# Head distances from two fp32r products with dA split in a high and a low part, in a two-layer hybrid decoder trunk

## The chip, the cores and the metric

One core of a Trainium2 chip. The metric is the device time of one execution in microseconds. The kernel before ran in 1644.17 us (median of 3 runs, 1643.96 to 1645.16).

## The reference

A decoder trunk of two layers on 256 tokens with 1024 features, all in float32. A layer is a half-step SwiGLU FFN, a mixer (an mLSTM branch with 4 heads beside a Mamba-2 SSD branch with 32 heads in 4 groups), a second FFN, and a gated per-layer embedding. The part that the change touches is the decay between positions in the SSD branch, in chunks of 128 tokens:

```python
acs = jnp.cumsum((dt * a_neg).reshape(bsz, nc, L, ng, ne), axis=2)
ah = jnp.transpose(acs, (0, 1, 3, 4, 2))
causal = jnp.tril(jnp.ones((L, L), dtype=bool))
decay = jnp.exp(jnp.where(causal, ah[..., :, None] - ah[..., None, :], -jnp.inf))
cb = jnp.einsum('bctgn,bcsgn->bcgts', cc, bc)
y_intra = jnp.einsum('bcgts,bcgets,bcsgep->bctgep', cb, decay.astype(x.dtype), xw)
...
y_inter = (jnp.einsum('bctgn,bcgepn->bctgep', cc, s_start.astype(x.dtype))
           * jnp.exp(acs)[..., None].astype(x.dtype))
```

## The kernel before

The five engines have one instruction list each, written out by hand, and meet at semaphores; there is no planner. SyncE loads weights. TensorE (PE) does the products, ScalarE (ACT) and VectorE (DVE) convert and evacuate, GpSimd (POOL) does a few masks and products.

**Units.** All weights come in units of 1 MB in a ring of three. For each unit ACT makes the rounded high part w_hi (L499, fp32r) and DVE the rest w_lo (L787); PE then computes three fp32r products for each block, hi by hi, hi by lo and lo by hi (`feat` L1316, `tok` L1328 to L1330 with 256 columns; `wide` and `tall` through L1342 to L1344 with 512). A unit of 48 instructions in the mixer is `feat` or `tok`.

**A layer's mixer** has 4 groups, `body(g, first)`, the first of which is written out and the others run in a loop. A group is 9 units: BC, QK, X01, X23, V, Z0, Z1, O, GA. Between them PE does the small work of the group. G counts the groups over both layers. Units 2 ahead are converted by `step(p)` on ACT and DVE.

**Distances.** dA = -softplus(dt) * exp(a_log) stands for all tokens and heads in one tile (DVE L931, once a layer, in `softplus_gates`). For chunk c and half (four heads of the group's eight) POOL builds R = tri_le * dA, 128 by 512 float32 (`distances_of` L402 to L406; the instruction is L404). PE multiplies it by the strict triangle (`segments` L1479, the product is L1482) and gets the sums of dA between two positions in bank 4 + 2c + half; ACT's exp (`decay` L599, L602) turns them into seg. For chunk 1 PE also multiplies by ones (`from_start` L1485, product L1488), which gives the sums from the chunk's start; ACT's exp (L610) makes cs. All these products have float32 operands. The two tiles R lie in the memory of xwe and of zth.

**Order around it in a steady group** (the second to fourth of a layer). On POOL: the tiles of chunk 0 were built at the end of the group before, after `yi_done` and `zth_ready` (L451 to L455); those of chunk 1 follow when `seg_done` says that PE has read chunk 0 (L431 to L433). Then the masks pm (L438), seg (L444) and cs (L448), the ysum addition (L458) after `ysq_ready`, and small copies for the next group (L413 to L419). On PE (L1583 to L1608): `segments(0,0)` in the middle of the second half of QK, `segments(0,1)` behind QK, `segments(1,0)` within X01, `segments(1,1)` behind it, the scores, X23, the first half of V, `from_start`, the rest of V, and so on; `outputs(1)` behind O signals `y_done`. On DVE: w_lo of X01 and X23, evacuation of BC, its convolution (L994 and L997: eight instructions on SBUF tiles), q and k (L1053, L1055), w_lo of V, the score distances pm (L1024, after PE's scores), w_lo of Z0, evacuation and convolution of X01, and so on; V's evacuation is L1067; at the end L1148 and L1153 make y. On ACT: tanh of the first convolution (L597), w_hi of V, exp of chunk 0, w_hi of Z0, tanh, exp of chunk 1.

**In the first group** of a layer the list is another: `small` and `small_back` bring the gate inputs, DVE's `softplus_gates` makes dA, PE waits for it in `gates` (L1453, L1454), then DVE does w_lo of V, `gate_rows` (L935 to L963: copies, scans and small steps on 4 partitions), w_lo of Z0, X01. POOL builds chunk 0 right after `dA_ready`. ACT copies cst (L667), which PE's `memory_read` (L1527) takes.

Merging after the groups (L1639 to L1651) runs `feat` on ha_hi, ha_lo and on yb_hi, yb_lo, which lie at `base` in the memory that the group's tiles had.

Of the kernel before, what the change touches and what calls it, by code (L numbers as in the profile page):

```python
# [5 lines left out]
F32 = mybir.dt.float32  # L6
F32R = mybir.dt.float32r
BF16 = mybir.dt.bfloat16
ALU = mybir.AluOpType
# [3 lines left out]
P = 128  # L13
# [10 lines left out]
def trunk(nc, T, out):  # L24
    DEPTH, D, FF = T["w1_ffn1"].shape
    S = T["x"].shape[1]
    CH = 128
    NC = S // CH
# [45 lines left out]
    with ctx:  # L74
# [4 lines left out]
        def at(name, shape, dt, off):  # L79
            n = 1  # L80
            for d in shape[1:]:
                n *= d
            n *= 2 if dt == BF16 else 4
            return nc.alloc_sbuf_tensor_at(name, shape, dt, offset=off), off + (n + 31) // 32 * 32

        def sb(name, shape, dt=F32):
            t, top[0] = at(name, shape, dt, top[0])
            return t

        raw = [sb(f"w_raw{i}", [P, KD, NP]) for i in range(RING)]  # L90
        whi = [sb(f"w_hi{i}", [P, KD, NP], F32R) for i in range(RING)]
# [14 lines left out]


        ident = sb("ident", [P, P])
        tri_le = sb("tri_le", [P, P])
# [9 lines left out]
        spx = sb("spx", [P, NC, 36])  # L119
        dA = sb("dA", [P, NC, SH])  # L120
        e_a = sb("e_a", [P, SH])
        dcol = sb("dcol", [P, SI // P])
# [26 lines left out]
        a = base  # L149
        seg, a = at("seg", [P, NC, EH, P], F32, a)  # L150
        xcv, a = at("xcv", [P, 4, S], F32, a)
        bcv, a = at("bcv", [P, 2, S], F32, a)
# [5 lines left out]
        cth, a = at("cth", [P, 2, S], F32, a)  # L158

        late = a  # L160
        xw, a = at("xw", [P, NC, EH * HP], F32, a)
        xwe, a = at("xwe", [P, EH * HP], F32, a)
# [5 lines left out]
        st, a = at("st", [P, EH * HP], F32, a)  # L168
        xin, a = at("xin", [P, 2, 2, S + 3], F32, a)
        zth, a = at("zth", [P, 2, S], F32, a)  # L170
        R = (xwe[:, :].rearrange("p (e t) -> p e t", e=4),
             zth[:, :, :].rearrange("p a b -> p (a b)").rearrange("p (e t) -> p e t", e=4))
        vtok, a = at("vtok", [P, NC, 258], F32, a)
# [25 lines left out]

        a5 = late  # L200
        r_i, a5 = at("r_i", [MH, S], F32, a5)
        r_f, a5 = at("r_f", [MH, S], F32, a5)
        r_b, a5 = at("r_b", [MH, S], F32, a5)
        r_w, a5 = at("r_w", [MH, S], F32, a5)
        pre_row, a5 = at("pre_row", [40, S], F32, a5)
        sp_a, a5 = at("sp_a", [P, NC, 36], F32, a5)
# [26 lines left out]
        def rows(x):  # L233
# [7 lines left out]
             u_hi_ready u_lo_ready silu_done prod_done h1_hi_ready h1_ready small_done x_abs sp_exp  # L241
            dA_ready ea_ready cum_done cum_exp row_tr row_ready row_back tok_ready r_built seg_done exp_done
            conv_done tanh_done cv_ready scores_done d_ready p_exp pm_ready sct_ready cb_done cbm_done
# [131 lines left out]
        def _(pool):  # L375
# [23 lines left out]
            def row_norm(n):  # L399
                power(n + 1, "var_ready", var[:, :], "rms_ready", rms[:, :])  # L400

            def distances_of(g, c, half):  # L402

                g_.tensor_tensor(R[half][:, :, :], tri_le[:, :].unsqueeze(1).broadcast_to([P, 4, P]),  # L404
                                 dA[:, c, bass.ds(g * EH + 4 * half, 4)].unsqueeze(2).broadcast_to([P, 4, P]),
                                 ALU.mult).then_inc(sem["r_built"], 1)  # L406

            def group(lay, g, first, last):
# [16 lines left out]
                if first:  # L425
                    pool.wait_ge(sem["dA_ready"], lay + 1)
                    for half in range(2):
                        distances_of(g, 0, half)
                else:
                    token_columns()  # L430
# [20 lines left out]
                if not last:  # L451
                    pool.wait_ge(sem["yi_done"], G + 1)
                    pool.wait_ge(sem["zth_ready"], G * 2 + 2)
                    for half in range(2):
                        distances_of(g + 1, 0, half)  # L455

# [317 lines left out]
        def _(dve):  # L774
# [120 lines left out]
            def softplus_gates(lay):  # L895
# [23 lines left out]
                for n in (15, 13, 11, 9, 7, 5, 3):  # L919
# [12 lines left out]
                                        in1=e_a[:, :].unsqueeze(1).broadcast_to([P, NC, SH]),  # L932
                                        op0=ALU.mult, op1=ALU.mult).then_inc(sem["dA_ready"], 1)

            def gate_rows(lay):  # L935
# [240 lines left out]

            dve.wait_ge(sem["const_ready"], 2)
            for c in range(NC):
                dve.wait_ge(sem["in_loaded"], 16 * NC)
                dve.sem_inc(sem["h_ready"], 2)  # L1180
# [113 lines left out]
        def _(pe):  # L1294
# [172 lines left out]
            def groups(lay):  # L1467
                def body(g, first):
# [10 lines left out]
                    def segments(c, half):  # L1479

                        pe.wait_ge(sem["r_built"], G * 4 + (2 * c + half + 1))
                        mm(bank[4 + 2 * c + half][:, :], tri_gt[:, :], R[half][:, :, :], start=True, stop=True)\  # L1482
                            .then_inc(sem["seg_done"], 1)

                    def from_start():  # L1485
                        for half in range(2):
                            pe.wait_ge(sem["exp_done"], G * 4 + (3 + half))
                            mm(bank[6 + half][:, :], ones[:, :], R[half][:, :, :], start=True, stop=True)\  # L1488
                                .then_inc(sem["seg_done"], 1)
# [259 lines left out]
```

## Time and profile before

| | |
|---|---|
| median of 3 runs | 1644.17 us (1643.96 to 1645.16) |
| time of the profiled execution | 1645.88 us |
| its span, first to last instruction | 1644.1 us |
| busy: PE, DVE, ACT, POOL | 1601.2, 1047.4, 730.1, 205.4 us |
| mean granted TensorE clock | 0.994 |

Busy time is the time in which an engine has an instruction running. Matmuls overlap, so for PE the distance from one start to the next tells what an instruction costs, not its own duration.

### The profile page before, as it was taken

What the parts mean: (1) busy time and instruction counts of PE and PEld (TensorE: products, weight loads), DVE (VectorE), ACT (ScalarE), POOL (GpSimd) and SP (SyncE); (2) the same over time, 40 slices, a digit from 0 to 9 for tenths busy, and PEclk for the clock granted to TensorE, in tenths of its full rate; (3) what the DMA queues carried; (4) which work ended last, traced back from release to release, by engine and by line L of the source; (5) the groups of instructions that cost most, each with busy time, mean ns of one, the idle gap of its engine ahead of it and who ended that gap; (6) DMA issues with size and microseconds to landing.
All of it is one profiled execution on the core that took longest, in us unless ns stands there. A gap on an engine that the chain in (4) does not pass through costs nothing.

```text
span 1644.1 us, 24426 instructions
## 1 busy us (share of the span) xinstructions
PE 1601.2 (97%) x9792; PEld 1399.9 (85%) x9792; DVE 1047.4 (64%) x1282; ACT 730.1 (44%) x880; POOL 205.4 (12%) x178
## 2 busy tenths in 40 slices
PE   7999989999999999999999999999999999999997
PEld 5888878999999978888778887899999999788885
DVE  5445488878777645454665545888787765554545
ACT  5444444444345345443554345344444543544444
POOL 1000013353330000000000000243343200000000
PEclk9999999999999999999999999999999999999999
DMA  7565634454545556555455654345453465466551
GB/s 238 182 201 179 171 111 129 129 165 126 170 128 180 180 166 198 194 184 184 157 186 184 193 179 142 115 129 153 156 152 117 140 204 193 149 203 197 184 180 64
DMA packets 245237, 270.85 MB, mean 165 GB/s; under 512 B 12504, under 2 KB 226360, under 8 KB 245176
## 3 DMA queue, kind: packets, MB, share of 16 engines
q1 hardware_dynamic: 239472, 266.90, 52.0%
q10 hardware_dynamic: 5704, 3.13, 0.7%
q8 instruction: 40, 0.66, 0.2%
q14 instruction: 21, 0.17, 0.0%
HBM read 268.94 MB, written 1.05 MB: 164 GB/s over the span
## 4 chain that ended last, share of the span: by engine, by line
PE 90%; DVE 5%; ACT 2%; issue 2%; DMA 0%; POOL 0%; SPq 0%; POOLq 0%; DVEq 0%; ACTq 0%
PE bank L1316 31%; PE bank L1342 16%; PE bank L1343 16%; PE bank L1344 16%; PE bank L1482 1%; DVE w_lo L787 1%; PE bank L1384 1%; PE bank L1330 1%; PE bank L1329 1%; PE bank L1328 1%; PE bank L1686 1%; ACT w_hi L499 1%; DVE xcv L997 1%; PE bank L1544 1%; PE bank L1488 1%
## 5 line engine op out<-in xcount | busy, mean ns | idle before, releaser
L787 DVE TENSOR_TENSOR w_lo<-w_raw,w_hi 128x2048 fp32r<-128x2048 f32 x252 | 586.8, 2330 | 292.4 <-ACT w_hi L499 292.4
L499 ACT ACTIVATE w_hi<-w_raw 128x2048 fp32r<-128x2048 f32 x252 | 481.3, 1913 | 228.8 <-PE bank L1344 116.2
L1316 PE MATMUL bank<-u_hi,w_hi 128*128 128x256 f32 x1152 | 341.7, 297 | 2.5 <-DVE u_lo L822 2.5
L1316 PE MATMUL bank<-u_lo,w_hi 128*128 128x256 f32 x1152 | 328.1, 285 | 0.0
L1316 PE MATMUL bank<-u_hi,w_lo 128*128 128x256 f32 x1152 | 328.1, 285 | 0.0
L1316 PEld LDWEIGHTS bank<-u_hi,w_hi 128*128 128x128 f32 x1152 | 223.1, 194 | 9.3 <-issue 7.8
L1316 PEld LDWEIGHTS bank<-u_lo,w_hi 128*128 128x128 f32 x1152 | 223.3, 194 | 5.1 <-issue 4.8
L1316 PEld LDWEIGHTS bank<-u_hi,w_lo 128*128 128x128 f32 x1152 | 223.0, 194 | 0.0
L1342 PE MATMUL bank<-w_hi,u_hi 128*128 128x512 f32 x416 | 166.8, 401 | 5.5 <-DVE u_lo L822 4.1
L1342 PE MATMUL bank<-w_hi,ha_hi 128*128 128x512 f32 x416 | 165.1, 397 | 3.5 <-DVE w_lo L787 3.4
L1344 PE MATMUL bank<-w_hi,u_lo 128*128 128x512 f32 x416 | 163.4, 393 | 0.0
L1343 PE MATMUL bank<-w_lo,u_hi 128*128 128x512 f32 x416 | 163.0, 392 | 0.0
L1344 PE MATMUL bank<-w_hi,ha_lo 128*128 128x512 f32 x416 | 162.5, 391 | 0.0
L1343 PE MATMUL bank<-w_lo,ha_hi 128*128 128x512 f32 x416 | 162.0, 390 | 0.0
L397 POOL TENSOR_TENSOR rms<-var,m_half 128x2 f32<-128x2 f32 x11 | 7.7, 696 | 1074.5 <-DVE var L815 1061.3
L1342 PE MATMUL bank<-w_hi,h_hi 128*128 128x512 f32 x352 | 139.1, 395 | 0.4
L1343 PE MATMUL bank<-w_lo,h_hi 128*128 128x512 f32 x352 | 138.5, 393 | 0.0
L1344 PE MATMUL bank<-w_hi,h_lo 128*128 128x512 f32 x352 | 136.9, 389 | 0.0
L553 ACT ACTIVATE h_hi<-bank 128x512 fp32r<-128x512 f32 x44 | 26.3, 598 | 165.4 <-PE bank L1384 165.4
L1342 PEld LDWEIGHTS bank<-w_hi,u_hi 128*128 128x128 f32 x416 | 78.7, 189 | 22.1 <-DVE w_lo L787 5.9
L1342 PEld LDWEIGHTS bank<-w_hi,ha_hi 128*128 128x128 f32 x416 | 78.1, 188 | 21.0 <-DVE w_lo L787 5.3
L1344 PEld LDWEIGHTS bank<-w_hi,u_lo 128*128 128x128 f32 x416 | 78.7, 189 | 17.0
(260 smaller groups left out, 2496.5 us busy)
## 6 DMA issues: line engine op xcount, KB each, us to landing
w_raw<-in_w_ffn_dram SPq DMA_DIRECT2D x264, 512.0 KB, 4.4
w_raw<-in_w_in_dram SPq DMA_DIRECT2D x160, 512.0 KB, 4.8
w_raw<-in_w_branch_b_dram SPq DMA_DIRECT2D x32, 512.0 KB, 4.1
w_raw<-in_w_branch_a_dram SPq DMA_DIRECT2D x16, 512.0 KB, 4.4
w_raw<-in_w_out_dram SPq DMA_DIRECT2D x16, 512.0 KB, 4.0
w_raw<-in_w_ple_gate_dram SPq DMA_DIRECT2D x16, 512.0 KB, 4.3
y_feat<-in_w_ple_dram ACTq DMA_DIRECT2D x2, 1024.0 KB, 5.1
h<-in_x_dram SPq DMA_DIRECT2D x2, 512.0 KB, 4.8
```

The source lines that it names most:

```text
L499: a_.activation(whi[slot][:, :, :], raw[slot][:, :, :], ACT.Copy).then_inc(sem["w_hi"], 1)
L553: a_.activation(h1_hi[b][:, :, :], two(6 - 2 * b), ACT.Copy).then_inc(sem["h1_hi_ready"], 1)
L787: v_.tensor_tensor(wlo[slot][:, :, :], raw[slot][:, :, :], whi[slot][:, :, :].bitcast(F32), ALU.subtract).then_inc(sem["w_lo"], 1)
L997: ins = v_.scalar_tensor_tensor(out=dst[:, q, :], in0=src, scalar=gcw[:, j, t:t + 1], in1=dst[:, q, :], op0=ALU.mult, op1=ALU.add)
L1316: i = mm(o, w[slot][:, k, cs], x[:, k, :], start=(k + q == 0 and not seeded), stop=(k == KD - 1 and q == 2 and not seeded), skip_group_che ...
L1328: mm(o, xh[:, k, cs], whi[slot][:, k, :], start=(k == 0), stop=False)
L1329: mm(o, xh[:, k, cs], wlo[slot][:, k, :], start=False, stop=False)
L1330: i = mm(o, xl[:, k, cs], whi[slot][:, k, :], start=False, stop=(k == KD - 1))
L1342: mm(o, xh, wh, start=start, stop=False, skip_group_check=True)
L1343: mm(o, xh, wl, start=False, stop=False, skip_group_check=True)
L1344: return mm(o, xl, wh, start=False, stop=stop, skip_group_check=True)
L1384: i = nc.tensor.transpose(bank[6 - 2 * b][:, k * S + c * P:k * S + (c + 1) * P], h1f[:, c, k * P:(k + 1) * P], ident[:, :])
```

## The change

dA is split, once a layer, in dA_hi, rounded to fp32r, and dA_lo, the rest rounded. The strict triangle and ones get fp32r copies. POOL builds R_hi and R_lo in place of R, and PE makes two fp32r products for each float32 one. R_hi lies where R lay (xwe and zth), R_lo in xw's memory. xw is read by `outputs`, so for the next group's chunk 0 POOL builds R_lo only after `y_done`. The gate rows that lay in xw's memory go to xcv's. The new operands of PE are placed at 64 modulo 256 bytes, and all that lies behind them moves.

```diff
+        def place(off, n):
+            return off + (n - off) % 256
...
+        top[0] = place(top[0], 64)
+        tri_gt_r = sb("tri_gt_r", [P, P], F32R)
+        ones_r = sb("ones_r", [P, P], F32R)
         ident = sb("ident", [P, P])
...
         dA = sb("dA", [P, NC, SH])
+        dA_hi = sb("dA_hi", [P, NC, SH], F32R)
+        dA_lo = sb("dA_lo", [P, NC, SH], F32R)
...
+        a = place(a, 64)
         late = a
+        xwe_at = late + NC * EH * HP * 4
...
+        a = place(a, 64)
+        zth_at = a
         zth, a = at("zth", [P, 2, S], F32, a)
-        R = (xwe[:, :].rearrange("p (e t) -> p e t", e=4),
-             zth[:, :, :].rearrange("p a b -> p (a b)").rearrange("p (e t) -> p e t", e=4))
+        R_hi = [at(f"R_hi{b}", [P, 4, P], F32R, off)[0] for b, off in enumerate((xwe_at, zth_at))]
+        R_lo = [at(f"R_lo{b}", [P, 4, P], F32R, late + b * 4 * P * 4)[0] for b in range(2)]
...
-        a5 = late
+        a5 = xcv_at
         r_i, a5 = at("r_i", [MH, S], F32, a5)
...
+            def part_of(dst, part, g, c, half):
+
+                return g_.tensor_tensor(
+                    dst[half][:, :, :], tri_le[:, :].unsqueeze(1).broadcast_to([P, 4, P]),
+                    part[:, c, bass.ds(g * EH + 4 * half, 4)].bitcast(F32).unsqueeze(2).broadcast_to([P, 4, P]), ALU.mult)
+
             def distances_of(g, c, half):
-                g_.tensor_tensor(R[half][:, :, :], tri_le[:, :].unsqueeze(1).broadcast_to([P, 4, P]),
-                                 dA[:, c, bass.ds(g * EH + 4 * half, 4)].unsqueeze(2).broadcast_to([P, 4, P]),
-                                 ALU.mult).then_inc(sem["r_built"], 1)
+                part_of(R_hi, dA_hi, g, c, half)
+                part_of(R_lo, dA_lo, g, c, half).then_inc(sem["r_built"], 1)
...
-                    pool.wait_ge(sem["dA_ready"], lay + 1)
+                    pool.wait_ge(sem["dA_split"], lay + 1)
...
                     for half in range(2):
-                        distances_of(g + 1, 0, half)
+                        part_of(R_hi, dA_hi, g + 1, 0, half)
+                    pool.wait_ge(sem["y_done"], G + 1)
+                    for half in range(2):
+                        part_of(R_lo, dA_lo, g + 1, 0, half).then_inc(sem["r_built"], 1)
...
+                dve.wait_ge(sem["dA_ready"], lay + 1)
+                ch.add(v_.tensor_copy(dA_hi[:, :, :], dA[:, :, :]))
+                ch.wait()
+                v_.tensor_tensor(dA_lo[:, :, :], dA[:, :, :], dA_hi[:, :, :].bitcast(F32), ALU.subtract)\
+                    .then_inc(sem["dA_split"], 1)
...
+            ch.add(v_.tensor_copy(tri_gt_r[:, :], tri_gt[:, :]))
+            ch.add(v_.tensor_copy(ones_r[:, :], ones[:, :]))
...
-                        mm(bank[4 + 2 * c + half][:, :], tri_gt[:, :], R[half][:, :, :], start=True, stop=True)\
+                        mm(bank[4 + 2 * c + half][:, :], tri_gt_r[:, :], R_hi[half][:, :, :], start=True, stop=False)
+                        mm(bank[4 + 2 * c + half][:, :], tri_gt_r[:, :], R_lo[half][:, :, :], start=False, stop=True)\
                             .then_inc(sem["seg_done"], 1)
...
-                            mm(bank[6 + half][:, :], ones[:, :], R[half][:, :, :], start=True, stop=True)\
+                            mm(bank[6 + half][:, :], ones_r[:, :], R_hi[half][:, :, :], start=True, stop=False)
+                            mm(bank[6 + half][:, :], ones_r[:, :], R_lo[half][:, :, :], start=False, stop=True)\
                                 .then_inc(sem["seg_done"], 1)
```

By the sizes of the tiles, `base` lies at 128 modulo 256 bytes before and at 0 after; the weights' ring, u_hi, u_lo, ha_hi and ha_lo stay at 192.

## Rows read from the trace of the kernel before

**Rows 1.** The page's chain that ended last, share of the span by engine.
```profile
PE 90%; DVE 5%; ACT 2%; issue 2%; DMA 0%; POOL 0%; SPq 0%; POOLq 0%; DVEq 0%; ACTq 0%
```

**Rows 2.** PE's groups by line (busy us, mean ns); then its timeline (start, length).
```profile
L1482 PE MATMUL bank<-xwe,tri_gt 128*128 128x512 f32 x32 | 16.4, 592 | 0.0
L1488 PE MATMUL bank<-xwe,ones 128*128 128x512 f32 x16 | 8.8, 631 | 0.0
...
254.98 1.02 PE L1482 MATMUL bank<-xwe,tri_gt 128*128 128x512 f32 x2
...
256.70 0.50 PE L1496 MATMUL bank<-bcv 128*128 128x128 f32 x3
```

**Rows 3.** PE's waits: for whom, us in total, times, longest.
```profile
PE bank L1454 <- DVE dA L931: 7.6, 2, 3.8
PE bank L1337 <- DVEq L1180: 6.9, 1, 6.9
```

**Rows 4.** PE's timeline in an FFN, the first and the 35th of 35 starts.
```profile
21.23 0.39 PE L1343 MATMUL bank<-w_lo,u_hi 128*128 128x512 f32 x1
...
28.98 0.39 PE L1344 MATMUL bank<-w_hi,u_lo 128*128 128x512 f32 x1
```

**Rows 5.** POOL's and DVE's timeline in a steady group; in brackets idle time and releaser.
```profile
367.56 1.17 POOL L404 TENSOR_TENSOR xwe<-tri_le,dA 128x512 f32<-128x512 f32 x1 [3.52 <-PE bank L1482]
369.83 1.04 POOL L404 TENSOR_TENSOR zth<-tri_le,dA 128x512 f32<-128x512 f32 x1 [1.10 <-PE bank L1482]
...
367.87 4.21 DVE L997 SCALAR_TENSOR_TENSOR bcv<-xin,gcw,bcv 128x256 f32<-128x256 f32 x6
...
378.09 0.61 DVE L1024 TENSOR_SCALAR pm<-bank,gtk 128x128 f32<-128x128 f32 x2 [1.23 <-PE bank L1504]
378.62 2.28 DVE L787 TENSOR_TENSOR w_lo<-w_raw,w_hi 128x2048 fp32r<-128x2048 f32 x1
...
382.31 2.71 DVE L997 SCALAR_TENSOR_TENSOR xcv<-xin,gcw,xcv 128x256 f32<-128x256 f32 x6
```

**Rows 6.** First groups: timeline of POOL and DVE; the last row is layer 1.
```profile
235.90 3.02 POOL L404 TENSOR_TENSOR xwe<-tri_le,dA 128x512 f32<-128x512 f32 x1 [11.63 <-DVE dA L931]
238.89 1.15 POOL L404 TENSOR_TENSOR zth<-tri_le,dA 128x512 f32<-128x512 f32 x1
...
235.60 0.22 DVE L931 SCALAR_TENSOR_TENSOR dA<-spx,e_a 128x64 f32<-128x64 f32 x1
235.74 2.28 DVE L787 TENSOR_TENSOR w_lo<-w_raw,w_hi 128x2048 fp32r<-128x2048 f32 x1
238.71 1.60 DVE L943 TENSOR_TENSOR_SCAN r_b<-ones,r_f 4x128 f32<-4x128 f32 x2
240.79 0.41 DVE L947 TENSOR_TENSOR_SCAN r_m<-r_w 4x128 f32<-4x128 f32 x1
255.18 0.88 DVE L1067 TENSOR_SCALAR vtok<-bank,rms 128x256 f32<-128x256 f32 x2 [1.33 <-PE bank L1330]
...
1064.56 0.88 DVE L1067 TENSOR_SCALAR vtok<-bank,rms 128x256 f32<-128x256 f32 x2 [0.35 <-PE bank L1330]
```

**Rows 7.** ACT's timeline in two steady groups; then a piece of the chain.
```profile
310.42 1.91 ACT L499 ACTIVATE w_hi<-w_raw 128x2048 fp32r<-128x2048 f32 x1 [0.34 <-PE bank L1316]
...
376.28 1.91 ACT L499 ACTIVATE w_hi<-w_raw 128x2048 fp32r<-128x2048 f32 x1 [0.76 <-PE bank L1316]
...
386.61 1.91 PE bank L1488 x4
```

**Rows 8.** PE by stretches behind the wait for dA: us, busy, granted clock, DMA share, GB/s.
```profile
236.00:242.00 6.00, 6.00 (x29) 0.50 0.48 120
1047.00:1053.00 6.00, 6.00 (x40) 0.72 0.54 170
```

**Rows 9.** The chain in order of time, merging of layer 0 (start, us, what).
```profile
513.35 5.75 PE bank L1316 x48
...
519.33 16.63 PE bank L1316 x144
```

More of the change, by code:

```diff
@@ L150, in trunk @@
         seg, a = at("seg", [P, NC, EH, P], F32, a)
+        xcv_at = a
         xcv, a = at("xcv", [P, 4, S], F32, a)
@@ L204, in trunk @@
         r_w, a5 = at("r_w", [MH, S], F32, a5)
+        assert a5 == xcv_at + 4 * S * 4
+        a5 = late + 4 * S * 4
         pre_row, a5 = at("pre_row", [40, S], F32, a5)
@@ L241, in trunk @@
              u_hi_ready u_lo_ready silu_done prod_done h1_hi_ready h1_ready small_done x_abs sp_exp
-            dA_ready ea_ready cum_done cum_exp row_tr row_ready row_back tok_ready r_built seg_done exp_done
+            dA_ready dA_split ea_ready cum_done cum_exp row_tr row_ready row_back tok_ready r_built seg_done exp_done
             conv_done tanh_done cv_ready scores_done d_ready p_exp pm_ready sct_ready cb_done cbm_done
```

## The prediction

> **What bounds the kernel now.** I read the chain that ended last first: TensorE (PE) carries 90% of it and VectorE (DVE) 5% [rows 1]. So a microsecond of PE work taken away is a microsecond gained wherever nothing else is due at the same moment. The whole argument is about where that holds. The matmuls to be replaced stand in [rows 2]: L1482 has 64 instructions and L1488 32 (the group on xwe is shown, that on zth has the same count), two for each float32 product, so 48 products: six in each of the 8 groups, four for `segments`, two for `from_start`. The list of PE's waits [rows 3] has nothing of the steady groups (the second to fourth of a layer): there PE seems never to wait, and its only large wait in the mixer is for dA, once a layer (the 6.9 us of L1337 are the input at the start). I then went through one steady group in order of time on DVE, ScalarE (ACT) and GpSimd (POOL) to see how much air lies under PE, and that changed my answer.
>
> **The PE side of the change.** In the middle of a stream a float32 product of 512 columns holds PE for 0.86 us: two of them fill 254.98 to 256.70 [rows 2]. A product of fp32r operands with 512 columns comes every 0.228 us: from 21.23 to 28.98 there are 34 steps [rows 4]. Two of them are 0.46 us, so each of the 48 saves 0.40 us, 19.4 us in all, if PE were free to take it. The Trainium skill (TensorE: Matmul & The Clock Gate, Back-to-back issue gap) puts an isolated matmul at columns/2.4 plus 2.5 ns, 216 ns for 512. The row says 228 ns, and I use the row; by the page the saving would be an estimated 20.5 us.
>
> **The POOL side.** R becomes R_hi and R_lo, so POOL makes 64 builds where it made 32, at 1.04 us when nothing is in its way [rows 5]. What counts is what a build does to DVE. In a steady group six of DVE's convolution steps (L997) take 4.21 us from 367.87 on, beside the builds at 367.56 and 369.83. The same six steps without a build take 2.71 us, from 382.31 on [rows 5]. So two builds cost DVE 1.5 us, each about 0.75, a little more where the whole build falls among short steps; I use 0.77. The reverse also shows: the build at 235.90 took 3.02 us, because it stood behind the w_lo that ran to 238.02 [rows 6], and that w_lo kept its length. So a long DVE instruction delays POOL, and a run of short ones is delayed by POOL. The Trainium skill (GPSIMD Engine Reference) says that GpSimd shares its SBUF interfaces with VectorE and contends with instructions that have two SBUF inputs; the rows agree with that sentence for L997, and it speaks against this change, which doubles the builds.
>
> **Steady groups (six of them).** The chunk-1 builds of a group follow `seg_done` of chunk 0, just when DVE does the first convolution. Four builds in place of two take 1.54 us more from it. Behind that convolution hangs ACT: tanh, w_hi, two exponentials, then w_hi at 376.28 after only 0.76 us of idle [rows 7]. That w_hi comes 1.54 - 0.76 = 0.8 us later and DVE's w_lo (L787) moves from 378.62 to about 379.04, by 0.4 us. DVE now waits 1.23 us for PE's scores before L1024 [rows 5]; that wait goes, since PE comes 1.6 us sooner and DVE 1.54 us later. Behind this w_lo stand the evacuation of X01, the convolution, the tanh, the exponentials of chunk 1, and for those `from_start` waits. In the kernel before, PE reaches `from_start` at 386.61, and its four instructions took 1.91 us there instead of the 1.72 of two products [rows 7]: exp and PE already arrive together. So the 1.6 us that PE gains on four `segments` products turn into a wait for exp_done: `from_start` begins 0.4 us later than now, not 1.6 us sooner. Its own pair then needs about 1.05 us (the second product waits for the second exponential, 0.53 us behind the first), saving 0.85 us. Net 0.45 us saved in such a group. In the first steady group ACT's idle is only 0.34 us [rows 7], so 0.1 us; in the third about as in the second. That is 0.9 us a layer, **-1.8 us** for both. After `from_start` I find air: DVE and ACT work ahead for Z1 and O, and the next wait of PE on them is for hn, which has no changed product before it.
>
> The builds for the next group move in part behind `y_done` (R_lo lies in xw, which `outputs` reads). Queued behind that wait on POOL is only the ysum addition, which waits for the square of y anyway and so for `y_done`. PE wants these tiles half a unit into QK, over 10 us later. The DVE steps next to them either read PSUM (L1148) or are one long instruction (L1153). I cost this at nothing; if it were exposed, two builds by 0.77 us would be 1.5 us a group, less ACT's idle of about 0.8.
>
> **First groups (two of them).** Here DVE is the tight engine. dA_hi and dA_lo are two small instructions with a wait, each about like the dA one itself (0.22 us [rows 6]): 0.5 us ahead of w_lo. POOL's builds now wait for dA_split, that much later; PE's own wait for dA (L1454) stays on dA_ready. The two copies of constants at the start fall into PE's 6.9 us of waiting for the input [rows 3]: nothing, 0.4 us at most. The four chunk-0 builds then stand behind that w_lo: the first ends near 239.4, the others near 242.7, in time for PE at 245.0. But `gate_rows` on DVE runs beside them. Now one build (238.89) overlaps it, and the two scans take 1.60 us, where one scan alone takes 0.41 [rows 6]: 0.78 us lost. Three overlap after: 2.3 us, 1.5 more. With the split, the next w_lo is 2.0 us late. The four chunk-1 builds then fall behind this w_lo and so nearly whole into the convolution of X01: another 1.7 us. DVE's list is thus 3.7 to 3.9 us late, against air of 1.33 us ahead of L1067 in the first layer and 0.35 in the second [rows 6], and 0.2 us at the tanh: L1067 starts 2.3 us and 3.5 us later than now. From L1067 the last chain runs over DVE's w_lo, the slow convolution of X23 (beside the masking on POOL) and the tanh to cst, which PE takes at L1527; DVE and ACT have no air there. So both first groups end later by that: **+5.8 us**, and the six shorter products there bring nothing.
>
> **Clock.** PE then waits some 5 us in two pieces in each first group. After its wait for dA the granted clock was 0.50 over 236 to 242 in layer 0 and 0.72 over 1047 to 1053 in layer 1 [rows 8], the lower level (1.2 GHz) for all or half of it, with no more idle ahead of it than this. I add **+1.3 us**, from 0 to 5.
>
> **Placement.** The tiles added ahead of `base` move it from 128 to 0 modulo 256 bytes, and with it yb_hi and yb_lo, which stream through 768 matmuls. The rows differ by tile: 48 instructions on ha took 5.75 us, 0.120 each, and the 144 after them, 96 on yb and 48 on ha again, 16.63 us [rows 9]; with 5.75 us for the 48, yb takes 0.113 each. What offset 0 gives no row shows. Bounds: 0.120 (+5 us) and 0.107, the 256 columns alone at 2.4 GHz (-5 us). I take 0, since no row speaks for one side.
>
> **Sum.** -1.8 + 5.8 + 1.3 = +5.3 us. The profiled execution has a span of 1644.1 us and a time of 1645.88; the median of the three timed runs is 1644.17. I add the difference to the median: **1649.5 us**.
>
> **Rivals.**
> - *No contention in the new builds* (they slip between DVE's instructions). Against: the two L997 rows of [rows 5] and the scans. DVE's list is then at its old time, PE takes 1.1 us of the four products plus 0.85 in a steady group (0.7 us and 0.85 in each first of them), 11 us in all, and 0.8 us in the first groups, where L1067 can move up by no more than DVE's air less the split: 1632. It can't reach the full 19.4 (1625), since from scores to `from_start` the length is DVE's and ACT's. Chance 0.1.
> - *Half the contention* (0.35 to 0.4 us a build, as when a build fits beside a semaphore wait of DVE's small steps). Steady groups save 1.1 us each, 6.6; the first groups lose 0.6 and 1.6: 1640. Chance 0.2.
> - *POOL itself is late* (slower on the other side than the forecast): a build that writes fp32r, or three of them blocked one after another behind w_lo, takes 2.1 us and more. Then r_built of the first group comes near 246.5 to 247, after PE's 245.0, and chunk 1 likewise in X01. It decides as soon as four builds after w_lo need over 6.5 us. Some 1.5 us in each group on top of the forecast for part of them: 1655. Nothing in the rows makes POOL slower for a type. Chance 0.1.
> - *The product doesn't get cheaper* (fp32r run as float32): against it stand 34 steps of 0.228 us. Then 1.6 us a group are lost on top: 1660. Chance 0.02.
> - The forecast itself, with clock and placement open, 1643 to 1656: 0.58.
>
> **How the numbers follow.** 0.2% of this time is 3.3 us, about what its measurement can tell. Faster than 1640.9: the first rival (0.1), over half of the second, and a little of the forecast with lucky placement: 0.23. Within: the rest of the second and the low end of the forecast, 0.17. Slower: 0.60. The range for 8 in 10 goes from 1637 (half contention and a gain by placement) to 1657 (forecast with the clock and placement against it, or POOL late).
>
> **What would show it.** PE's two products at L1482 and L1488 at some 0.23 us each, twice as many builds at L404's successor. In the list of PE's waits: new waits of `from_start` for ACT's seg exponentials, 1.5 to 2 us in each of six groups, and of the transposes or L1527 for xcv and cst in the first groups, 2 us or more. L997 on bcv in a steady group, 4.21 us now, at about 5.7. Steady group periods 65.9 us now, near 65.4 after. If instead those six steps stay near 4.2 us, or PE shows no wait at `from_start`, my prediction is wrong and the time lies near 1632 to 1640. If yb's matmuls leave 0.113 us, the placement moved the time, not the change.

## The result, and the profile after

The changed kernel runs in 1666.63 us (median of 4 runs, 1665.84 to 1668.11) beside 1644.62 us for the kernel before: ratio 1.0136, interval 1.012 to 1.0152. The forecast was 1649.5 with a range to 1657, so its sign held and its size did not: +22 us, not +5.3. The profiled execution took 1665.84 us with a span of 1664.0, 19.9 us longer than before.

I cut both spans at the same marks on PE: the product that waits for dA, the transposes of hn, the product for y's variance, and the first product of the per-layer embedding. Lengths in us; "periods" are the six distances between the hn transposes of one steady group and the next.

| stage | before | after |
|---|---|---|
| start to dA of layer 0 (FFN and first products) | 235.9 | 237.2 |
| embedding of layer 0 to dA of layer 1 | 451.7 | 453.4 |
| embedding of layer 1 to the end | 239.9 | 241.2 |
| first group, dA to hn, layer 0 and 1 | 48.3, 47.1 | 52.6, 52.4 |
| steady periods | 65.8 65.9 65.8, the same in layer 1 | 66.4 67.2 65.2, 66.4 67.3 65.3 |
| fourth hn transposes to y's variance, each layer | 12.0 | 12.0 |
| y's variance to embedding (merging), each layer | 101.0 | 102.7 |

The differences: +4.3 in the first three rows, +9.6 in the first groups, +2.7 in the six periods, +3.4 in merging; 20.0 in all. The first three rows and merging hold no changed product at all.

The share of the chain that ended last, by engine, kernel after; it answers to [rows 1]:

```profile
PE 70%; DVE 14%; issue 7%; POOL 4%; ACT 3%; DMA 0%; ACTq 0%; POOLq 0%; DVEq 0%
```

PE had 90%. DVE, and POOL behind it, now carry part of the mixer. The share alone doesn't measure the loss: in a version below that is 32 us faster than this one (e10) PE's share is 70% too. PE's waits, kernel after (us in total, times, longest), beside [rows 3]:

```profile
PE bank L1519 <- ACT seg L625: 13.0, 6, 2.7
PE bank L1484 <- DVE dA L954: 7.6, 2, 3.8
PE bank L1367 <- DVEq L1210: 6.8, 1, 6.8
PE bank L1553 <- DVE xcv L1036: 5.7, 2, 2.8
...
PE bank L1559 <- ACT cst L690: 4.5, 2, 2.2
```

L1519 is `from_start`, L1553 the transposes of xcv, L1559 the old L1527. Three waits are new or grown, 23 us together: the first stands in each steady group, the two others in each first group. The products themselves did get cheap. PE's timeline in the first group (start, length), where [rows 2] had two in 1.72 us:

```profile
245.18 0.39 PE L1512 MATMUL bank<-R_hi,tri_gt_r 128*128 128x512 f32 x1
245.41 0.40 PE L1513 MATMUL bank<-R_lo,tri_gt_r 128*128 128x512 f32 x1
245.64 0.39 PE L1512 MATMUL bank<-R_hi,tri_gt_r 128*128 128x512 f32 x1
245.87 0.39 PE L1513 MATMUL bank<-R_lo,tri_gt_r 128*128 128x512 f32 x1
```

They start 0.23 us apart. DVE and POOL from the end of one group to the first convolution of the next (start, length, idle time and releaser), kernel after; the later rows answer to [rows 5]:

```profile
360.97 1.24 DVE L1181 SCALAR_TENSOR_TENSOR y_feat<-xcv,zs 128x1024 f32 x1 [0.17 <-DVE xcv L1176]
362.14 1.39 DVE L1188 TENSOR_SCALAR osg<-osg,ghn 128x256 f32<-128x256 f32 x2
...
373.63 0.69 DVE L1011 TENSOR_TENSOR xin<-bank,rB 128x512 f32<-128x512 f32 x1
374.36 1.56 DVE L1022 TENSOR_SCALAR bcv<-xin,gcw,gcb 128x256 f32<-128x256 f32 x2
375.96 4.16 DVE L1025 SCALAR_TENSOR_TENSOR bcv<-xin,gcw,bcv 128x256 f32<-128x256 f32 x6
...
360.10 3.02 POOL L420 TENSOR_TENSOR R_lo<-tri_le,dA_lo 128x512 fp32r<-128x512 f32 x2
...
376.78 1.22 POOL L420 TENSOR_TENSOR R_lo<-tri_le,dA_lo 128x512 fp32r<-128x512 f32 x1
```

Two of these steps in the kernel before, that on osg and the convolution's first two:

```profile
355.29 0.61 DVE L1160 TENSOR_SCALAR osg<-osg,ghn 128x256 f32<-128x256 f32 x2
...
367.10 0.73 DVE L994 TENSOR_SCALAR bcv<-xin,gcw,gcb 128x256 f32<-128x256 f32 x2
```

So the R_lo builds behind `y_done` (360.10 to 363.1) stretch L1188 by 0.8 us, and those of chunk 1 (373.69 to 378.0) stretch L1022 by another 0.8. The stretch of L1188 stands at two of the three turns of a layer; at the third (into the last group) the step takes 0.61 us as before. In the first group (kernel after, DVE then POOL), beside [rows 6]:

```profile
237.40 0.22 DVE L960 TENSOR_TENSOR dA_lo<-dA,dA_hi 128x64 fp32r<-128x64 f32 x1
237.54 2.28 DVE L810 TENSOR_TENSOR w_lo<-w_raw,w_hi 128x2048 fp32r<-128x2048 f32 x1
...
242.15 1.08 DVE L973 TENSOR_TENSOR r_w<-r_i,r_b 4x256 f32<-4x256 f32 x1
243.27 1.15 DVE L975 TENSOR_TENSOR_SCAN r_m<-r_w 4x128 f32<-4x128 f32 x1
...
251.62 4.15 DVE L1025 SCALAR_TENSOR_TENSOR xcv<-xin,gcw,xcv 128x256 f32<-128x256 f32 x6
...
258.20 0.87 DVE L1095 TENSOR_SCALAR vtok<-bank,rms 128x256 f32<-128x256 f32 x2
...
245.88 4.50 POOL L420 TENSOR_TENSOR R_hi<-tri_le,dA_hi 128x512 fp32r<-128x512 f32 x1 [1.75 <-PE bank L1513]
```

Counted from dA (start of its DVE step: 235.60 and 236.91), vtok's evacuation comes at 19.58 us before and 21.29 after; DVE's idle ahead of it is gone. What follows on PE in windows, kernel after (us, busy, granted clock, DMA share, GB/s):

```profile
272.00:284.00 12.00, 8.76 (x50) 0.72 0.60 173
276.33:282.33 6.00, 6.00 (x28) 0.54 0.99 278
...
394.50:398.50 4.00, 4.00 (x24) 0.58 0.00 0
```

In the kernel before the first of these stretches was at full clock:

```profile
272.00:284.00 12.00, 11.05 (x109) 1.00 0.85 231
```

The first two are around and behind the waits for xcv (2.85 us, to 272.99) and cst (2.24 us, to 276.33), the last is behind `from_start`'s wait of 2.10 us in the second steady group. In each PE runs in part at the lower level (1.2 GHz). What of this falls into the wait for cst costs nothing; in the 6 us behind it 0.46 of 6 us is 2.7 us lost (in layer 1 the clock there is 0.58, 2.5 us), and 0.42 of 4 us is 1.7 us lost.

### The profile page after: what moved, and what is told of

It reads as the page before. It is cut to its first block, busy times and chain, and to the rows that moved or that the text cites. A ratio compares the mean times of both kernels' runs of the same rounds, so it can differ in the third digit from the quotient of the medians.

```text
span 1664.0 us, 24480 instructions
## 1 busy us (share of the span) xinstructions
PE 1598.7 (96%) x9792; PEld 1408.2 (85%) x9792; DVE 1069.0 (64%) x1288; ACT 728.8 (44%) x880; POOL 258.4 (16%) x210
## 4 chain that ended last, share of the span: by engine, by line
PE 70%; DVE 14%; issue 7%; POOL 4%; ACT 3%; DMA 0%; ACTq 0%; POOLq 0%; DVEq 0%
PE bank L1346 17%; PE bank L1372 16%; PE bank L1374 16%; PE bank L1373 16%; DVE w_lo L810 3%; DVE xcv L1025 2%; DVE bcv L1025 2%; ACT w_hi L522 1%; POOL R_lo L420 1%; PE bank L1414 1%; POOL R_hi L420 1%; PE bank L1718 1%; DVE xcv L1022 1%; DVE xin L1011 1%; DVE bcv L1022 1%
## 5 line engine op out<-in xcount | busy, mean ns | idle before, releaser
L1346 PE MATMUL bank<-u_hi,w_hi 128*128 128x256 f32 x1152 | 335.1, 291 | 2.5 <-DVE u_lo L845 2.5
```

Source lines behind the costliest of these rows:

```text
L1346: i = mm(o, w[slot][:, k, cs], x[:, k, :], start=(k + q == 0 and not seeded), stop=(k == KD - 1 and q == 2 and not seeded), skip_group_che ...
```

## Experiments

**Placement.** The merging gave it away: nothing there was changed but addresses. Chain in order of time, merging of layer 0, kernel after (start, us, what), beside [rows 9]:

```profile
520.24 5.75 PE bank L1346 x48
...
526.23 17.05 PE bank L1346 x144
```

The 48 on ha still take 5.75; the 96 on yb take 17.05 - 5.75 = 11.30, .1178 each, where they took .1133. First test: the changed kernel with `base` back at 128, and the kernel before with `base` at 0.

```diff
-        base = top[0]
+        base = top[0] + 128
```

> The changed kernel with 128 bytes of padding ahead of base, so that yb and h1 lie again at 128 modulo 256 bytes as in the kernel before. Theory 'placement is a third of the loss': in the two traces 1056 matmuls with h1 as stationary went from 0.2291 to 0.2332 us (4.3 us) and 768 with yb as moving operand from 0.1135 to 0.1178 us (3.3 us), so this comes out 7.6 us under the changed kernel, near 1659. Rival 'the slower pace has another cause, such as traffic of POOL': both paces stay and the time stays near 1666.6.

> The kernel before with 128 bytes of padding ahead of base, nothing else. Theory 'placement': 7.6 us over the kernel before, near 1652.2, h1 at 0.2332 and yb at 0.1178 us, and no wait of PE that was not there. Rival: 1644.6, as before.

e1: 1657.34 us, ratio 1.0074 [1.0057, 1.0091], 9.3 us under the changed kernel. e2: 1653.41 us, ratio 1.0053 [1.0036, 1.007], with the old products and builds, 8.3 us over the kernel before. The stages moved as a block: e1 has 235.6, 451.6, 239.9 and 101.0 (those of before) and first groups and periods as after; e2 has 237.7, 453.8, 240.9 and 102.7 with periods of 65.9. In e1 the chain of merging reads:

```profile
518.71 5.75 PE bank L1346 x48
...
524.69 16.63 PE bank L1346 x144
```

The first three rows of the table have another tile at `base`, h1_hi and h1_lo of the FFN, as the stationary operand. Two starts of the same product twelve apart on PE's timeline, kernel after:

```profile
41.29 0.40 PE L1374 MATMUL bank<-w_hi,h_lo 128*128 128x512 f32 x1
...
44.09 0.40 PE L1374 MATMUL bank<-w_hi,h_lo 128*128 128x512 f32 x1
```

and e1:

```profile
40.69 0.39 PE L1374 MATMUL bank<-w_hi,h_lo 128*128 128x512 f32 x1
...
43.44 0.39 PE L1374 MATMUL bank<-w_hi,h_lo 128*128 128x512 f32 x1
```

2.80 against 2.75 us, .2333 against .229 a product. There are 3 x 352 of them, 1056 by .0041 = 4.3 us; yb gives 768 by .0043 = 3.3 us. Together 7.6 us, which the two runs confirm within their intervals. With the placement put back (e1) the change still costs 12.3 us, over twice the forecast.

What about the offset matters? Three runs shifted all tiles, ring and base alike, by 64, 128 and 192 bytes; for yb as the moving operand I then had theories by its own offset modulo 256.

```diff
-        top[0] = (top[0] + 63) // 64 * 64
+        top[0] = (top[0] + 63) // 64 * 64 + 64
```

> The kernel before with every tile 64 bytes higher: ring, u and ha at 0 modulo 256, base at 192. It asks what offset the fp32r matmuls of PE like, for moving and for stationary operands. If the moving operand's offset alone counts (192: 0.120 us for 256 columns, 128: 0.1135, 0: 0.118), the products on ring and u go to 0.118 and those of 512 columns down by 2 ns: near 1634. If the stationary operand counts alike (h1 at 0 was 0.2332 against 0.2291 at 128), 0 is bad there: near 1650.

> The kernel before with every tile 128 bytes higher: ring, u and ha at 64 modulo 256, base at 0, where yb and h1 are slower by 7.6 us as measured. If offset 64 is like 192 for the ring's products, 1652; if 64 is better, as the placement of the new tiles at 64 in the change may hint, under 1640.

> The kernel before with every tile 192 bytes higher: ring, u and ha at 128 modulo 256, base at 64. With the moving operand at 128 the 256-column products should come every 0.1135 us as yb did (3456 on u, 384 on ha and 384 of tok by 6.5 ns: 27 us less) and the 512-column ones gain some 6 ns (3552: 21 us): near 1600. Rival: the pace depends on the pair of offsets, both operands at 128 is as slow as both at 192: 1644.

All three were misses for those theories: 1645.03, 1644.49 and 1644.54 us, ratios 0.9998, 0.9994 and 0.9998, with every pace as before; only the rival named for e7, that the pair of offsets counts, came out. An operand's own offset changed nothing; what is left is its difference to the other operand, the weights in the ring. Then u and ha, whose products run at .1198 with a difference of 0 to the weights, were put where yb was:

```diff
+        top[0] += 192
         h = sb("h", [P, NC, D])
...
-        base = top[0]
+        base = top[0] + 64
```

> The kernel before with two pads and nothing else: the tiles behind the ring (h, u_hi, u_lo, ha_hi, ha_lo) move by 192 bytes, so u and ha lie 64 below the ring's offset modulo 256, as yb did before; base keeps its offset, so yb stays where it was against the ring. Theory (the pair of offsets of the two operands sets the pace, by yb's three cases): the products of 256 columns on u and ha go from .1198 to about .1135 us each. There are 3456 and 384 of them, 24.2 us; where u is the stationary operand under 512 columns, the pace may go from .2277 to .2291 as with h1 (about 2500 of them, 3.5 us back). Time near 1624, ratio 0.987. Rival (u's and ha's pace has another cause than the offset, the layout of their columns or the weights beside them): 1644, paces unchanged. Second rival (the sign is another for u, since h1 showed the opposite roles): .1178, near 1637 to 1640.

1639.53 us, ratio 0.997 [0.9957, 0.9982]: faster, but by 5 us, not 20. Two units of u products, 24 steps apart, in e9:

```profile
332.81 0.28 PE L1317 MATMUL bank<-u_hi,w_lo 128*128 128x256 f32 x1
335.53 0.28 PE L1317 MATMUL bank<-u_hi,w_lo 128*128 128x256 f32 x1
...
342.07 0.28 PE L1317 MATMUL bank<-u_lo,w_hi 128*128 128x256 f32 x1
344.89 0.28 PE L1317 MATMUL bank<-u_lo,w_hi 128*128 128x256 f32 x1
```

The first runs at .1133, the next at .1175, and so it goes on, unit by unit, with no unit at .1198. By the mean steps of the trace u and ha gave 15.6 us and not 24; 4.0 went back on the products of 512 columns, about as expected, 3.3 on yb and 3.1 into longer waits of PE. And yb, whose difference had not changed modulo 256, was now at .1178; merging took 101.5. Was its place the cause, 256 bytes further up? One run moved `base` alone by 256:

```diff
-        base = top[0]
+        base = top[0] + 256
```

> The kernel before with base moved by 256 bytes and nothing else, so that yb lies 448 instead of 192 above the ring modulo 1024, the same modulo 256; u and ha stay at 0. In the run with u and ha moved, yb had this place and its products took .1178, not .1135. Theory (only the difference modulo 256 counts, and the .1178 there came from something passed on by the products on ha, which were at .1178 too): yb .1135, merging 101.0 us, time 1644 to 1645, ratio 1.000. Rival (the place counts over more than 256 bytes; modulo 1024 every kernel so far fits, with .1135 at 192 and 960 and .1178 at 320, 448 and 832): yb .1178, merging 102.7, time 1648 to 1653, ratio 1.002 to 1.005.

1644.70 us, ratio 1.0 [0.999, 1.0009], yb at .1135, merging 101.0. So the place isn't the cause. What holds in all runs: difference 0 gives .1198; another difference gives .1135 or .1178, a whole unit at one or the other. In the twelve kernels with u and ha at difference 0, yb was at .1135 with -64 bytes (eight kernels) and at .1178 with +64 (four: the changed one, e2, e3, e4), in all units of both layers. Once the products in front of yb leave .1198 the level isn't fixed by the offset alone: in e11 below, with the same differences as e9, yb is at .1135. What picks the level stays open.

**The R_lo builds.** POOL makes 32 more builds. They can be left out while PE keeps its two products (it multiplies R_hi twice, so the low part of dA is missing from the distances):

```diff
-                part_of(R_hi, dA_hi, g, c, half)
-                part_of(R_lo, dA_lo, g, c, half).then_inc(sem["r_built"], 1)
+                part_of(R_hi, dA_hi, g, c, half).then_inc(sem["r_built"], 1)
...
-                        mm(bank[4 + 2 * c + half][:, :], tri_gt_r[:, :], R_lo[half][:, :, :], start=False, stop=True)\
+                        mm(bank[4 + 2 * c + half][:, :], tri_gt_r[:, :], R_hi[half][:, :, :], start=False, stop=True)\
```

> The changed kernel without the builds of R_lo (and without the wait for y_done that belongs to them); PE multiplies R_hi twice, so the low part of the distances is left out and the high part counts twice. PE's work is that of the changed kernel, POOL's that of the kernel before. Theory 'the second builds take DVE's time': the waits at from_start shrink from 13.0 us to about 2, those in the first groups vanish, and with base still at 0 the time is near 1652 - 12 = 1640. Rival 'PE's new products themselves, or the split of dA, cost': the time stays over 1655.

1642.86 us, ratio 0.9987 [0.9978, 0.9997], with `base` still at 0. First groups 47.3 and 47.3, periods 63.9 to 64.1, PE's waits:

```profile
PE bank L1555 <- ACT cst L686: 4.5, 2, 2.2
PE bank L1515 <- ACT seg L621: 2.5, 6, 0.6
PE bank L1549 <- DVE xcv L1032: 0.8, 2, 0.4
```

The waits of 13.0 and 5.7 us shrink to 2.5 and 0.8 without the builds; that for cst stays at 4.5, so the builds aren't what makes it. The 32 builds cost 24 us, with the slow clock that came behind their waits: 10.4 in the first groups, 13.9 in the periods. The other way round, all builds stay and PE multiplies dA's tile in float32 (R_lo is built and not read):

```diff
-                        mm(bank[4 + 2 * c + half][:, :], tri_gt_r[:, :], R_hi[half][:, :, :], start=True, stop=False)
-                        mm(bank[4 + 2 * c + half][:, :], tri_gt_r[:, :], R_lo[half][:, :, :], start=False, stop=True)\
+                        mm(bank[4 + 2 * c + half][:, :], tri_gt[:, :], R_hi[half][:, :, :], start=True, stop=True)\
```

> The changed kernel with all its builds, but R_hi holds dA itself in float32 and PE makes the old float32 product from it (R_lo is built and not read). Theory 'the length is DVE's and ACT's, not PE's': the products cost 19 us of PE more, but they fall into its waits: the time is within 4 us of the changed kernel, 1664 to 1671, and from_start's wait is under 1 us a time. Rival 'PE's saving is really in the changed kernel and something else ate it': 1666.6 + 19 = 1686.

1669.2 us, ratio 1.0144 [1.0127, 1.0161], an interval that overlaps that of the changed kernel. The cheaper product, 19.4 us of PE work, is worth 0 to 3 us as long as the builds are there. The wait at `from_start` was 5.4 us in all, 1.3 the longest, a little above the 1 us expected: even the old product arrives early.

Which builds? This run has `base` at 128 and leaves out only those behind `y_done` (PE takes R_hi twice for chunk 0 of steady groups, the low part is missing there):

> The changed kernel with base at 128 modulo 256 (as in the run that padded it, 1657.3) and without the R_lo builds behind y_done: for chunk 0 of the steady groups PE multiplies R_hi twice, so the low part is left out there. In a steady group two of six builds are gone, those beside y. Theory 'these builds are not free, as the prediction had it': in the changed kernel DVE's evacuation of BC stood 1.0 us later against PE than before, from L1188 and from POOL's small copies behind a w_lo; so 1 us less in each of six groups and most of the half-clock stretches behind from_start's wait, together 6 to 9 us: near 1650. Rival 'ACT's idle absorbs them, only the chunk-1 builds count': 1657.

1651.77 us, ratio 1.0038 [1.0024, 1.0052], against 1657.34 for e1. Periods 65.5, 65.3, 65.3, where e1 has 66.4, 67.2, 65.2: 5.6 us over six. Its waits for seg are 1.93, 1.76 and 1.65 us a layer, those of e1 2.70, 2.09 and 1.64. PE's stretch behind the second of these, in e1:

```profile
393.00:397.00 4.00, 4.00 (x24) 0.57 0.00 0
```

and in e8:

```profile
392.00:396.00 4.00, 4.00 (x37) 1.00 0.00 0
```

So 1.7 us a layer of those 5.6, 3.4 in all, is the clock, and 2.2 the builds' own. The third period is the same in both, as L1188 isn't stretched ahead of it. The six periods of e8 are 392.1 us, those of e3 383.9: the R_lo builds of chunk 1 cost the other 8.2.

**A version that keeps the gain.** ScalarE builds R_lo, four activations a tile, each the triangle scaled by one column of dA_lo; POOL builds R_hi alone. `base` is at 128. The result is the full computation.

```diff
+                def low_part(g, c, half):
+                    for e in range(4):
+                        i = a_.activation(R_lo[half][:, e, :], tri_le[:, :], ACT.Copy,
+                                          scale=dA_lo[:, c, bass.ds(g * EH + 4 * half + e, 1)].bitcast(F32))
+                    i.then_inc(sem["r_lo"], 1)
...
+                        pe.wait_ge(sem["r_lo"], G * 4 + (2 * c + half + 1))
```

> The changed kernel with base back at 128 and with R_lo built by ScalarE (four activations a tile, each the triangle times one column of dA_lo) and not by GpSimd. GpSimd then makes 32 builds as in the kernel before, and all products stay. Theory (GpSimd's extra builds beside VectorE's short SBUF steps are the loss, in first groups and steady ones): first groups at 47 to 48.5 us from dA to hn, steady periods 64 to 64.5, merging 101.0, in all 1635 to 1638, ratio 0.9945 to 0.996; the kernel that had no R_lo at all, with its base at 0, took 1642.9, and placement is worth 7 to 9. Rival (ScalarE is as tight as VectorE there, so that eight or more activations a group land on the chain to the exponentials): 1645 or more, with waits for seg of over 2 us a time.

1634.68 us, ratio 0.9943 [0.9927, 0.996]: 10 us under the kernel before, 32 under the change, and at the low end of what was expected. First groups 47.3 and 48.8 (in the second the clock fell behind the wait for cst), periods 63.8 to 64.1, merging 101.0. ScalarE is not the new bound. In e10, ACT, DVE and POOL around the turn of a group:

```profile
348.16 2.44 ACT L606 ACTIVATE R_lo<-tri_le,dA_lo 128x128 fp32r<-128x128 f32 x8
...
352.15 1.23 DVE L1197 SCALAR_TENSOR_TENSOR y_feat<-xcv,zs 128x1024 f32 x1 [0.17 <-DVE xcv L1192]
353.30 0.61 DVE L1204 TENSOR_SCALAR osg<-osg,ghn 128x256 f32<-128x256 f32 x2
...
364.01 0.69 DVE L1027 TENSOR_TENSOR xin<-bank,rB 128x512 f32<-128x512 f32 x1
364.74 1.33 DVE L1038 TENSOR_SCALAR bcv<-xin,gcw,gcb 128x256 f32<-128x256 f32 x2
366.10 3.50 DVE L1041 SCALAR_TENSOR_TENSOR bcv<-xin,gcw,bcv 128x256 f32<-128x256 f32 x6
```

The step on osg is back at 0.61, y_feat to xin takes 11.86 us where it took 12.66 in the changed kernel (12.23 in the one before), and the convolution is 0.9 us shorter. PE's waits in e10:

```profile
PE bank L1576 <- ACT cst L701: 4.5, 2, 2.2
...
PE bank L1536 <- ACT seg L627: 2.4, 6, 0.6
```

With u and ha moved as in e9 on top:

> The one before (R_lo built by ScalarE) together with u and ha 64 below the ring. If both effects hold and add, 20 us under it: near 1615, ratio 0.982. If faster products on u and ha only turn into waits for ScalarE's and VectorE's conversion of the weights (w_hi 1.9 us and w_lo 2.3 us a unit of 48 products, 5.75 us now and 5.45 then, so there is air), less: 1620 to 1625. If the layout does nothing, 1636.

1632.55 us (1628.96 to 1635.16), ratio 0.9923 [0.9904, 0.9941]. The interval overlaps that of e10, so the layout's own share, some 2 us, is not shown; its waits for seg grew from 2.4 to 8.3 us, so part of the faster products turned into waiting. No run of e11 was near the 1615 that full addition would give.

## Why the prediction was wrong, by its own steps

| step | forecast | runs |
|---|---|---|
| steady groups | -1.8 | +2.7, of it +3.4 clock |
| first groups, DVE late | +5.8 | +4.6 |
| clock in the first groups | +1.3 | +5.3 |
| placement | 0 | +7.6 |
| sum | +5.3 | +20.2 |

The stages give 20.0: the first groups grew by 9.6, where the two rows for them, read each by itself, add up to 9.9. The forecast failed in four terms: the placement put at nothing, the builds behind `y_done` put at nothing, and the clock mis-sized in the first groups and left out in the steady ones.

**The products (right).** 0.23 us each, and by e4 worth next to nothing here, as I had argued from the air under `from_start`. The "no contention" rival had -11 us for steady groups; with the R_lo builds gone e3 shows 383.9 us for six periods against 395.1, -11.2. Its arithmetic was right, its condition was not met.

**The new waits (right in place, put a little too short).** All three stand where I put them. At `from_start` they are 1.66 to 2.70 us, not 1.5 to 2. The one for cst (2.2 us a layer) stands in e3 and e10 too, so late builds aren't its cause.

**Builds behind `y_done` (wrong).** "I cost this at nothing" is the step that failed in the steady groups. I looked at L1148 and L1153 as neighbours and passed over L1160, the two short steps on osg right behind them. They read and write SBUF, and the builds stretch them from 0.61 to 1.39 us at two of three turns. ScalarE's conversion and everything up to the evacuation of BC hang behind. The Trainium skill (SBUF — State Buffer, SBUF: two separate sides) says that the pair of ports shared with GpSimd is an exclusive lock, held for a whole instruction, and that it is taken by VectorE for two SBUF inputs or for a mode that uses both ports for one. I had looked only for two inputs, though the sentence of the Trainium skill that the prediction used names both cases. L1188 and L1022 have one SBUF tensor, and the trace (0.61 to 1.39, 0.73 to 1.56 us) agrees with the page's second case. The bound I gave for exposure, 1.5 us less ACT's idle of 0.8, was 4.2 us for six groups; e1 against e8 gives 5.6, of it 3.4 clock. Without these builds the steady groups stand at -3.0 (e8), near my -1.8 (a layer's terms, 0.1, 0.45 and 0.45, add up to 1.0 and not 0.9, so it should have read -2.0).

**The convolution (mechanism right, shared out otherwise).** I expected 5.7 us for L997's successor. It took 4.16, but the two L1022 steps ahead of it took 1.56 instead of 0.73. Both together are 5.7 us against 4.94: 0.8 more for two more builds, where I had 1.54. That comparison flatters the builds, since the old ones met other steps: in the first steady group it is 1.3, and e8 against e3 (the same place with and without R_lo builds of chunk 1) gives 1.4 in each, 0.7 a build. Spread over all four builds a build costs 0.57 us, over the two of before 0.75.

**First groups (right, a little high).** vtok's evacuation comes 1.7 us later in layer 0 (21.29 - 19.58) and 2.9 in layer 1, forecast 2.3 and 3.5. Three builds over the rows' steps did what was said: L973 took 1.08, L975 1.15, where their predecessors took 0.41 each. The forecast was 0.6 us too high in each layer.

**Clock (mis-sized).** I gave 1.3 us with 0 to 5. Behind the wait for cst it cost 2.7 us in layer 0 and 2.5 in layer 1, against none before: +5.3, just past my upper end. At the start of layer 0's group the clock was better than before, 0.83 over the 10 us from dA on against 0.70. That isn't the change's doing: e2 and e6, which keep the old builds and products, have 0.83 there too. It bears on DVE's lateness, 1.7 us in that layer and 2.9 in the other: in the kernel before, L1067 stood 1.2 us further behind dA in layer 0 than in layer 1. I priced the waits that I had found and hardly the slow stretch that can come after one, and I had none in the steady groups, where one wait of three had one behind it, and not the longest.

**Placement (wrong by being set to zero, and half of it not seen).** I found the difference between ha and yb in [rows 9], bounded it at 5 us either way and took the middle for lack of a sign. The sign was against, +3.3 us. And `base` carries more than yb: h1_hi and h1_lo lie there too, as stationary operands under 1056 products, another 4.3 us that stands in no step of mine. The case for a range as narrow as mine rested on one of two tiles.

Of the rivals, "half contention" isn't borne out: e8 against e3 gives 0.7 us a build, not 0.35 to 0.4, and e8's steady groups stand at -3.0, not -6.6. "POOL late" did not decide: in the first group the four builds were done at 244.1, before PE's 245.18. That the product doesn't get cheaper is refuted by the starts 0.23 us apart.

## What to carry to other kernels

Before moving work to POOL, list every DVE step on SBUF tiles beside it, one-input steps too, and price each build at what it takes from them; ScalarE did the same work in its idle time at no cost that shows (e10's periods are those of e3). When a change moves a base address, list all tiles behind it and each product that reads them, and look at the pace in steps that the change doesn't touch. A wait of 2 us on TensorE is to be priced together with the stretch at the lower clock that may follow it: here such a stretch cost 1.4 to 3.0 us (e4 has both ends).

## What the runs showed of the hardware that I had not expected

**The pace of a product depends on where its two operands lie to each other.** 256 columns: .1198 us at difference 0 modulo 256 bytes, .1135 or .1178 otherwise. 512 columns with h1 stationary: .2291 or .2333. Shifting everything by 64, 128 or 192 bytes changes nothing. The Trainium skill (TensorE: Matmul & The Clock Gate, Step-by-step: what each phase is for) says that loading the next weights doesn't steal read bandwidth from the running matmul; these paces, up to 5.5% apart for the same columns by the place of one operand against the other, are not what that would lead one to expect. Whether the loading of weights is what slows a product no run here isolates.

**The clock falls after some waits and not after others like them.** Behind the 3.8 us for dA it fell in every run. 2.70 us at `from_start` in the first steady group left it at 1.00, 2.10 us in the second brought 0.58. The wait of 2.24 us for cst had no fall around it in e3, where the wait for xcv 3 us ahead was 0.4 us, and had one in the changed kernel (that wait 2.85 us) and in e4 (0.85 us; granted clock 0.54 over 278 to 284). In e10, with 0.4 us for xcv and 2.24 for cst in both layers, it stayed up in layer 0 and fell in layer 1:

```profile
272.28:280.28 8.00, 8.00 (x66) 1.00 0.92 263
1075.35:1083.35 8.00, 8.00 (x51) 0.79 0.92 262
```

So the lengths of the waits don't tell these cases apart; no run here isolates what does.

**POOL pays too.** A build takes 1.04 us alone, 3.02 behind one w_lo, 4.50 when it met the one at 247.21, and small copies of four columns took 2.26 us behind w_lo.
